# Twelve weight pieces summed from direct cast loads in the gate stage, ten in the FFN units; LN1 scaling split over engines; output stores on SP

## The chip, the cores and the metric

One Trainium2 chip, 8 NeuronCores, each running the same program on one batch element of the input. A core has TensorE (PE, matmuls, with its weight loads as PEld), VectorE (DVE), ScalarE (ACT), GpSimd (POOL) and SyncE (SP), which here only issues DMAs. DMAs issued from SP move data as they are; DMAs issued from POOL can also cast float32 to bfloat16 on the way. A time is the device time, in microseconds (us), of the slowest core.

## What is computed

One encoder layer with post-norm residuals, width 1024, 2048 tokens a core:

```python
proj = x @ w_in                    # conv input, attention q k v, memory q, 3 x 1024 gate logits
y_conv, y_attn, y_mem = conv branch, windowed attention, memory attention
gates = sigmoid(gate_logits + b_gate).reshape(B, S, 3, D)
merged = gates[:, :, 0] * y_conv + gates[:, :, 1] * y_attn + gates[:, :, 2] * y_mem
x = layer_norm(alpha * x + merged @ w_o, ln1_g, ln1_b)
gate, up = split(x @ w_ffn_in, 2)  # 2 x 2816 columns
x = layer_norm(alpha * x + (silu(gate) * up) @ w_ffn_out, ln2_g, ln2_b)
```

## The kernel before

Each engine runs its instructions in the order in which the program emits them; the small class `Eng` (line 36) adds the semaphore waits that each instruction needs. So an instruction that waits holds up all that its engine was given later, and a DMA that waits holds up the engine that issues it. Line 148 issues every DMA, line 233 every matmul.

**Stage A** (to about 320 us): input projections, convolution, both attentions and the first quarter of the gates, in an order written out by hand (`ORDER`). In it POOL also casts pieces of `w_ffn_in` from float32 to a bfloat16 copy in DRAM (`cache_w1`, `w1_bf16_cache`), 8 times one piece and then, in `load_b`, three.

**Gate stage** (lines 980 to 1013, about 320 to 583 us). `c_main(dp, tt)` lists 12 items for one quarter `dp` of the columns and one block `tt` of 512 tokens: for two column halves and three branches a gate (`c_gate`, 8 matmuls, ACT applies tanh, line 838) and an output (`c_out`, 4 matmuls, DVE multiplies out of PSUM, line 859); POOL adds the three products (lines 866 and 871). Stage A holds `dp` 0, the gate stage `dp` 1 to 3, 144 items. Ahead of each quarter POOL issues the next quarter's weights (three `w_g`, one `w_out`). PSUM has 8 banks, taken in turn; five buffers `gb` hold gates.

In between, `straight` calls `fold_step` after every 6 items. The FFN's first product is done by Strassen's scheme: a unit (128 columns) has seven matmul groups of 4 matmuls of 512 columns on seven forms of its weights. A piece comes as four quarter blocks; five more forms are sums of these. `fold_load` (SP) reloads a piece from the DRAM copy, `fold_sum` adds the forms on DVE (lines 819 to 821) and SP stores seven forms to DRAM (`w1_forms`). 22 pieces, two buffers `FG`. The copies that stage A left out are issued by `cache_w1(4)`, `(4)` and `(3)` among the weight loads.

**w_o loop** (line 1295 on, 16 blocks of 128 tokens): `d_mm` (16 matmuls), `d_H` (residual add and sum, DVE, line 1073), and a pipeline step `d_chain`, which serves five blocks at once: transposes on PE (`d_Tpe`) and their copy on ACT (`d_Tev`, line 1112), the sum of squares on ACT (`d_S`, line 1032), three tiny DVE ops (`d_tiny`, lines 1037 to 1042), the reciprocal root on POOL (`d_rstd`, line 1047), and `d_C`: LN1's centring and scaling on DVE (lines 1052 and 1054), a cast to bfloat16 on ACT (line 1092), a store of x1 to DRAM. 12 of 20 steps run here, 8 more inside FFN units 0 to 10. Then `e_sums` forms the input sums of Strassen's scheme on DVE (lines 1138 to 1142).

**FFN**, twice (two halves of 1024 tokens): 22 units `f1_unit` (even: gate, odd: up), then 8 blocks `f2_block` (44 matmuls each, then the residual, LN2 and the output store). A unit's weights come from `w1_forms` into three buffers `w1s`; `load_w1(u + 2)` is issued at the start of unit u. In a unit ACT copies three products out of PSUM (line 1172), POOL adds them twice (lines 1179 and 1183), the last four groups accumulate onto these banks, and DVE subtracts and adds out of PSUM four times (line 1193). After a gate unit ACT applies SiLU (1198, 1201 and, later, 1223, 1226); in an up unit DVE (1207, 1211) and, after the next unit's adds, POOL (1232, 1236) multiply. The order of POOL and ACT in the next unit is set by the list `late`. While units 7 to 17 run, POOL casts `w_ffn_out` in (22 loads). `load_hb` reads x1 back as the residual.

## Time and profile before

| what | us |
|---|---|
| median of 3 runs (1131.66 to 1138.48) | 1133.59 |
| the profiled execution, device time | 1130.92 |
| its span on the slowest core (core 1) | 1129.4 |
| PE busy | 985.3 (87%) |
| DVE busy | 541.1 (48%) |
| ACT busy | 396.2 (35%) |
| POOL busy | 326.9 (29%) |
| DMA queue of POOL, share of 16 engines | 27.1% |
| DMA queue of SP, share of 16 engines | 30.7% |

The spans of the eight cores lie between 1117.6 and 1129.4 us. A busy PE is a PE with matmuls in flight: how fast they go depends on the granted clock, which a table by stage shows beside the busy time (1.00 is 2.4 GHz, 0.50 is 1.2 GHz). An idle engine costs something only where the chain of work waits for it, so waits are read from the stage in which PE stops.

### The profile page before, as it was taken

To read this page: it belongs to the slowest core of one execution; us is meant where nothing else is said; L and a number is where in the kernel's file an instruction comes from. 1 tells how busy PE (TensorE), PEld (TensorE's weight loads), DVE (VectorE), ACT (ScalarE), POOL (GpSimd) and SP (SyncE) were. 2 spreads that over 40 slices of the span, in tenths; PEclk is the share of its full clock that TensorE was granted. 3 is DMA by queue.
4 is the path that set the end of the run, shared out by engine and by line. 5 is a ranking of instruction groups with operands and counts; after the bars stand their busy time and mean duration, and the time that the engine had idled before them with its cause. 6 is when DMAs were issued, how large, how long until landed. Compare 5 with 4: busy or idle time off the path is not lost.

```text
span 1129.4 us, 16455 instructions; the slowest of 8 cores (1117.6 to 1129.4 us)
## 1 busy us (share of the span) xinstructions
PE 985.3 (87%) x5606; PEld 452.3 (40%) x5606; DVE 541.1 (48%) x949; ACT 396.2 (35%) x604; POOL 326.9 (29%) x346
## 2 busy tenths in 40 slices
PE   4999999898991589289999878799999989999996
PEld 1455545444440234034444323344444434444442
DVE  2223757476611143035637964535564445545344
ACT  1136575665520112012223644444411134443011
POOL 3200001021430133033320124467731145665111
PEclk9999999999995889689999988989999989999998
DMA  9994144543499969957538533589823354442132
GB/s 129 166 175 93 44 105 70 120 67 72 73 139 159 157 198 219 168 194 245 180 137 267 187 103 135 154 216 241 216 105 112 112 183 162 139 157 66 57 112 75
DMA packets 45586, 161.15 MB, mean 143 GB/s; under 512 B 5632, under 2 KB 17544, under 8 KB 44256
## 3 DMA queue, kind: packets, MB, share of 16 engines
q1 hardware_dynamic: 32096, 110.54, 30.7%
q0 software_dynamic: 13408, 49.55, 27.1%
q8 instruction: 47, 0.77, 0.3%
q14 instruction: 35, 0.29, 0.1%
HBM read 161.32 MB, written 50.65 MB: 188 GB/s over the span
## 4 chain that ended last, share of the span: by engine, by line
PE 64%; DMA 19%; DVE 6%; issue 6%; POOL 3%; ACT 2%; SPq 1%; DVEq 0%; ACTq 0%; POOLq 0%
PE ps L233 63%; DMA w_forms<-arena 10%; DMA arena<-w_bf_cache 4%; DMA arena<-xt 2%; DVE arena L1052 2%; DVE arena L1193 2%; DMA arena<-u_scratch 1%; DMA arena<-w_forms 1%; POOL arena L1179 1%; POOL arena L1183 1%; ACT arena L1172 1%; SPq L148 1%; DVE arena L1054 1%; POOL arena L148 0%; POOL arena L1236 0%
## 5 line engine op out<-in xcount | busy, mean ns | idle before, releaser
L233 PE MATMUL ps<-arena 128*128 128x512 bf16 (+5 forms) x5196 | 969.7, 366 | 131.7 <-DVE arena L859 68.4
L233 PEld LDWEIGHTS ps<-arena 128*128 128x128 bf16 (+2 forms) x5196 | 432.1, 99 | 651.9 <-issue 212.0
L1193 DVE TENSOR_TENSOR arena<-arena,ps 128x512 f32<-128x512 f32 x176 | 114.7, 682 | 143.7 <-POOL arena L1183 141.1
L838 ACT ACTIVATE arena<-ps,bgate_sb 128x512 f32<-128x512 f32 x96 | 65.8, 687 | 239.7 <-PE ps L233 236.5
L866 POOL TENSOR_TENSOR arena<-arena 128x512 f32<-128x512 f32 x32 | 40.8, 1275 | 212.5 <-DVE arena L859 212.5
L1172 ACT COPY arena<-ps 128x512 f32<-128x512 f32 x132 | 76.2, 585 | 68.4 <-PE ps L233 63.1
L1179 POOL TENSOR_TENSOR arena<-arena 128x512 f32<-128x512 f32 x44 | 55.8, 1268 | 124.4 <-ACT arena L1172 124.3
L859 DVE SCALAR_TENSOR_TENSOR arena<-arena,ps 128x512 f32<-128x512 f32 x96 | 63.6, 681 | 52.5 <-PE ps L233 48.5
L1032 ACT ACTIVATE arena<-arena 128x1024 bf16<-128x1024 f32 x32 | 33.8, 1057 | 156.3 <-DVE arena L1259 146.7
L819 DVE TENSOR_TENSOR arena<-arena 128x1024 bf16<-128x1024 bf16 x22 | 16.4, 745 | 133.9 <-DMA arena<-w_bf_cache 133.9
L148 POOL DMA_DIRECT2D arena<-w_g x21 | 11.3, 544 | 171.1 <-PE ps L233 169.9
L1183 POOL TENSOR_TENSOR arena<-arena 128x512 f32<-128x512 f32 x44 | 55.6, 1264 | 9.1 <-POOL arena L1179 9.1
L1047 POOL TENSOR_TENSOR mvt<-mvt,eps_t 128x1 f32<-128x1 f32 x32 | 17.7, 554 | 138.4 <-DVE mvt L1042 138.4
L871 POOL TENSOR_TENSOR arena<-arena 128x512 bf16<-128x512 f32 x32 | 43.2, 1350 | 28.5 <-DVE arena L859 24.3
L645 ACT ACTIVATE arena<-ps 128x1024 bf16<-128x1024 f32 x46 | 46.6, 1025 | 12.2 <-PE ps L233 11.9
L648 DVE TENSOR_TENSOR arena<-arena 128x1024 bf16<-128x1024 bf16 x46 | 33.8, 736 | 28.4 <-ACT arena L645 28.2
L1052 DVE SCALAR_TENSOR_TENSOR arena<-arena,mvt 128x1024 f32<-128x1024 f32 x32 | 41.0, 1282 | 13.2 <-POOL mvt L1047 13.2
L1054 DVE SCALAR_TENSOR_TENSOR arena<-arena,mvt 128x1024 f32<-128x1024 f32 x32 | 41.1, 1284 | 3.8 <-DVE arena L1052 0.5
L1259 DVE SCALAR_TENSOR_TENSOR arena<-arena,ps 128x1024 f32<-128x1024 f32 x16 | 19.5, 1221 | 44.5 <-PE ps L233 44.5
L1198 ACT ACTIVATE arena<-ps 128x512 f32<-128x512 f32 x22 | 13.1, 598 | 66.6 <-DVE arena L1193 66.6
L1092 ACT CAST arena<-arena 128x1024 bf16<-128x1024 f32 x16 | 16.7, 1045 | 44.6 <-DVE mvt L1037 37.7
L352 ACT CAST arena<-ps 128x512 bf16<-128x512 f32 (+1 forms) x32 | 18.3, 571 | 38.1 <-PE ps L233 38.1
(106 smaller groups left out, 546.3 us busy)
## 6 DMA issues: line engine op xcount, KB each, us to landing
arena<-w_forms SPq DMA_DIRECT2D x44, 896.0 KB, 5.1
w_forms<-arena SPq DMA_DIRECT2D x22, 896.0 KB, 6.0
arena<-w_bf_cache SPq DMA_DIRECT2D x22, 512.0 KB, 4.3
arena<-u_scratch SPq DMA_DIRECT2D x64, 135.0 KB, 3.7
arena<-x SPq DMA_DIRECT2D x16, 512.0 KB, 9.8
x_scratch<-arena SPq DMA_DIRECT2D x16, 512.0 KB, 3.0
arena<-x_scratch SPq DMA_DIRECT2D x16, 512.0 KB, 3.8
out<-arena POOLq DMA_DIRECT2D x16, 512.0 KB, 3.0
```

Source lines behind the costliest of these rows:

```text
L233: return pe.run(lambda: nc.tensor.matmul(out, lhsT, rhs, start=start, stop=stop, skip_group_check=onto), deps, inc)
L645: t_p = act.run(lambda: nc.scalar.activation(flat, bank2(b), AF.Exp, scale=0.125), [tk, PTw_free[rp], btab["t"]])
L838: t = act.run(lambda: nc.scalar.activation(gb[r], ps[:, bk, :], AF.Tanh, bias=bgate[:, b * 8 + dc:b * 8 + dc + 1], scale=0.5), [tk, gb_fre ...
L859: t_y = dve.run(lambda: nc.vector.scalar_tensor_tensor(out=gb[r], in0=gb[r], scalar=1.0, in1=ps[:, bk, :], op0=ALU.add, op1=ALU.mult), [tk ...
L866: c_state["s"] = pool.run(lambda: nc.gpsimd.tensor_tensor(out=gb[r0], in0=gb[r0], in1=gb[r], op=ALU.add), [c_state["y", 0], t_y])
L871: t_mg[dp, tt, dci] = pool.run(lambda: nc.gpsimd.tensor_tensor(out=merged[dp][:, dci, tt * 512:(tt + 1) * 512], in0=gb[r0], in1=gb[r], op= ...
L1052: te = dve.run(lambda: nc.vector.scalar_tensor_tensor(out=buf, in0=buf, scalar=mv[:, 0:1], in1=tabs[:, 0, :], op0=ALU.subtract, op1=ALU.mu ...
L1054: return dve.run(lambda: nc.vector.scalar_tensor_tensor(out=dst, in0=buf, scalar=mv[:, 2:3], in1=tabs[:, 1, :], op0=ALU.mult, op1=ALU.add) ...
L1172: return act.run(lambda: nc.scalar.copy(dst, ps[:, b, :]), deps)
L1179: s = pool.run(lambda: nc.gpsimd.tensor_tensor(out=T3, in0=T3, in1=T4, op=ALU.add), [t3, t4])
L1183: s1 = pool.run(lambda: nc.gpsimd.tensor_tensor(out=T1, in0=T3, in1=T1, op=ALU.add), [s, t1])
L1193: return dve.run(lambda: nc.vector.tensor_tensor(out=dst, in0=dst, in1=ps[:, b, :], op=op), deps)
```

## The change

- Twelve pieces are summed in the gate stage, one per 12 items: POOL loads a piece with a cast straight from the float32 weights into SBUF, in a `w_ffn_in` layout with the four blocks reordered, issued 18 items ahead; the seven forms now fill one buffer. The other ten pieces are all copied to DRAM in stage A (8 single ones, two in `load_b`), loaded as four blocks into the unit's weight buffer, and summed there by DVE at the end of the unit two before (`fold_w1(u + 2)`), in both passes. The copies in the gate stage go.
- LN1: the centred rows y are stored to DRAM instead of x1. Centring (`d_Y`) no longer waits for the reciprocal root. Scaling writes bfloat16 directly: on DVE for every third block and for all in the FFN units, else on ACT (scale) and POOL (add of the bias). The residual of LN2 is rebuilt from y on ACT and POOL ahead of each `f2_block` (`hb_prep`).
- The chain starts a block earlier and rests once: 14 steps in the w_o loop, 6 in the units. `e_sums` stands ahead of the last `d_H`. `w_ffn_out` loads begin at unit 8.
- LN2's table goes to buffers of its own, loaded after unit 21. Output stores are issued by SP.

The diff, cut to its core (left out: declarations, the host's reordering of the blocks, `cache_w1(2)` for `(3)` in `load_b`, the counter's start at piece 12, `z_free` as the first wait of a gate buffer):

```diff
@@ -801,33 +803,38 @@

-    FG = [V(156.5 + 9 * i, [128, 9, 4, 128]) for i in range(2)]
+    FG = [V(156.5 + 7 * i, [128, 7, 4, 128]) for i in range(2)]
     fg_slot = [new_slot("fg") for _ in range(2)]
...

-    def fold_load(v):
-        if v < 22:
-            fold_ld[v] = dma(sp, FG[v % 2][:, 0:4], w1b_d[v], fg_slot[v % 2], [w1_raw[v], fold_st.get(v - 2), a_done])
-
-    def fold_sum(v):
-        G = FG[v % 2].rearrange("p s k c -> p s (k c)")
+    def fold(buf, dep):
+        G = buf.rearrange("p s k c -> p s (k c)")

...

-        dve.run(lambda: nc.vector.tensor_tensor(out=G[:, 4:6, :], in0=G[:, 0:2, :], in1=twice(3), op=ALU.add), [fold_ld[v]])
-        dve.run(lambda: nc.vector.tensor_tensor(out=G[:, 6:8, :], in0=G[:, 0:2, :], in1=twice(2), op=ALU.add))
-        t = dve.run(lambda: nc.vector.tensor_tensor(out=G[:, 8, :], in0=G[:, 3, :], in1=G[:, 2, :], op=ALU.subtract))
-        fold_st[v] = dma(sp, w1f_d[v], FG[v % 2][:, 2:9], fs_slot[v % 2], [t])
-
-    fold_n = iter(range(22))
+        t1 = dve.run(lambda: nc.vector.tensor_tensor(out=G[:, 4:6, :], in0=G[:, 2:4, :], in1=twice(0), op=ALU.add), [dep])
+        dve.run(lambda: nc.vector.tensor_tensor(out=G[:, 6, :], in0=G[:, 1, :], in1=G[:, 0, :], op=ALU.subtract))
+        return dve.run(lambda: nc.vector.tensor_tensor(out=G[:, 2:4, :], in0=G[:, 2:4, :], in1=twice(1), op=ALU.add), [t1])
+
+    def fold_load(v):
+        if v < NFOLD:
+            fold_ld[v] = dma(pool, FG[v % 2][:, 0:4], w_f1_d[v], fg_slot[v % 2], [fold_st.get(v - 2), a_done])
+
+    def fold_sum(v):
+        t = fold(FG[v % 2], fold_ld[v])
+        fold_st[v] = dma(sp, w1f_d[v], FG[v % 2], fs_slot[v % 2], [t])
+
+    fold_n = {"i": 0}

     def fold_step():
-        v = next(fold_n, None)
-        if v is not None:
-            fold_load(v + 1)
-            fold_sum(v)
+        i = fold_n["i"]
+        fold_n["i"] += 1
+        if i % 12 == 5 and i >= 12:
+            fold_load(i // 12 + 1)
+        if i % 12 == 11:
+            fold_sum(i // 12)

...
@@ -890,11 +897,11 @@

-    def straight(items, each=0):
-        for i, (_, f) in enumerate(items):
+    def straight(items, folds=False):
+        for _, f in items:
             f()
             tick()
-            if each and i % each == each - 1:
+            if folds:
                 fold_step()
...
@@ -980,18 +987,16 @@
     a_done = pe.tok()
-    cache_w1(4)
+    fold_load(0)
     t_ln1 = load(ln1t, bass.AP(ln1_d.tensor, 0, [[0, 128], [D, 2], [1, D]]), [a_done, t_sT[3, 3]], sp)
-    fold_load(0)
     load_wg(2, [pe.tok()])
     load_wos(2, [])
-    cache_w1(4)
-    straight(cat([c_main(1, tt) for tt in range(4)]), 6)
+    fold_load(1)
+    straight(cat([c_main(1, tt) for tt in range(4)]), True)
     load_wg(3, [pe.tok()])
...
     t_wo = load(w_o_sb, w_o_d, [a_done])
-    cache_w1(3)
-    straight(cat([c_main(2, tt) for tt in range(4)]), 6)
+    straight(cat([c_main(2, tt) for tt in range(4)]), True)
     dp2_done = pe.tok()
...
@@ -1000,17 +1005,24 @@
     def load_w2(j):
-        w2_tok[j] = load(w2[j], w_f2_d[:, j, :], [x1_st[j // 2 + (12 if j < 8 else 0)]])
+        w2_tok[j] = load(w2[j], w_f2_d[:, j, :], x1_free[j // 2 + (12 if j < 8 else 0)])

...
         if u < 44:
-            r = u % 3
-            w1_tok[u] = dma(sp, w1s[r], w1f_d[u % 22], w1_slot[r], [w1_free[r], fold_st[u % 22]])
-
-    straight(cat([c_main(3, tt) for tt in range(4)]), 6)
+            r, v = u % 3, u % 22
+            if v < NFOLD:
+                w1_tok[u] = dma(sp, w1s[r], w1f_d[v], w1_slot[r], [w1_free[r], fold_st[v]])
+            else:
+                w1_tok[u] = dma(sp, w1s[r][:, 0:4], w1b_d[v], w1_slot[r], [w1_free[r], w1_raw[v]])
+
+    def fold_w1(u):
+        if u < 44 and u % 22 >= NFOLD:
+            w1_tok[u] = fold(w1s[u % 3], w1_tok[u])
+
+    straight(cat([c_main(3, tt) for tt in range(4)]), True)
     c_done = pe.tok()
...
@@ -1042,17 +1054,21 @@

-    def ln_rstd(t3, k):
-        mv = mvt[:, k % 4, :]
+    def ln_rstd(t3, k, out):
         return pool.run(lambda: nc.gpsimd.tensor_tensor(
-            out=mv[:, 2:3], in0=mv[:, 1:2], in1=eps_t[:, 2:3], op=ALU.pow), [t3, t_eps])
-
-    def ln_affine(buf, tabs, dst, t_rs, k, deps=()):
-        mv = mvt[:, k % 4, :]
-        te = dve.run(lambda: nc.vector.scalar_tensor_tensor(
-            out=buf, in0=buf, scalar=mv[:, 0:1], in1=tabs[:, 0, :], op0=ALU.subtract, op1=ALU.mult), [t_rs, deps])
+            out=out, in0=mvt[:, k % 4, 1:2], in1=eps_t[:, 2:3], op=ALU.pow), [t3, t_eps])
+
+    def ln_center(buf, tab, k, deps):
         return dve.run(lambda: nc.vector.scalar_tensor_tensor(
-            out=dst, in0=buf, scalar=mv[:, 2:3], in1=tabs[:, 1, :], op0=ALU.mult, op1=ALU.add), [te])
+            out=buf, in0=buf, scalar=mvt[:, k % 4, 0:1], in1=tab, op0=ALU.subtract, op1=ALU.mult), deps)
+
+    def ln_scale(buf, dst, rs, tab, deps):
+        return dve.run(lambda: nc.vector.scalar_tensor_tensor(
+            out=dst, in0=buf, scalar=rs, in1=tab, op0=ALU.mult, op1=ALU.add), deps)
+
+    def ln_scale_ap(buf, mid, dst, rs, tab, deps):
+        t = act.run(lambda: nc.scalar.activation(mid, buf, AF.Identity, scale=rs), deps)
+        return pool.run(lambda: nc.gpsimd.tensor_tensor(out=dst, in0=mid, in1=tab, op=ALU.add), [t])

...
@@ -1082,17 +1098,30 @@

+    Z = [V(184.5 + 4 * i, [128, D], F32) for i in range(2)]
+    z_free = [None, None]
+
+    def d_Y(tb):
+        xb = X1[tb % 12]
+        d_state["y", tb] = ln_center(xb, ln1t[:, 0, :], tb, [d_state["t3", tb], t_ln1])
+        x1_st[tb] = dma(sp, y_d[tb * 128:(tb + 1) * 128, :], xb, st_slot[tb % 12], [d_state["y", tb]])
+
     def d_rstd(tb):
-        d_state["rs", tb] = ln_rstd(d_state.pop(("t3", tb)), tb)
-
-    def d_C(tb):
+        d_state["rs", tb] = ln_rstd(d_state.pop(("t3", tb)), tb, rs16[:, tb:tb + 1])
+
+    def d_C(tb, on_dve):
         xb = X1[tb % 12]
         r = tb % 3
-        t_ln = ln_affine(xb, ln1t, xb, d_state.pop(("rs", tb)), tb, [t_ln1])
-        d_state["cb", tb] = act.run(lambda: nc.scalar.copy(x1b[r], xb), [t_ln, x1b_free[r]])
+        deps = [d_state["rs", tb], d_state.pop(("y", tb)), x1b_free[r], z_free[tb % 2]]
+        rs, b1 = rs16[:, tb:tb + 1], ln1t[:, 1, :]
+        if on_dve:
+            t_ln = ln_scale(xb, x1b[r], rs, b1, deps)
+        else:
+            t_ln = ln_scale_ap(xb, Z[tb % 2], x1b[r], rs, b1, deps)
+            z_free[tb % 2] = t_ln
+        d_state["cb", tb] = t_ln
         d_state["ln"] = t_ln
-        x1_st[tb] = dma(sp, x1_d[tb * 128:(tb + 1) * 128, :], xb, st_slot[tb % 12], [t_ln])
-        x1_free[tb] = [x1_st[tb], d_state["cb", tb]]
+        x1_free[tb] = [x1_st[tb], t_ln]
         if tb + 12 < 16:
...
@@ -1239,10 +1268,12 @@

+        fold_w1(u + 2)
+
     def load_hb(tb):
...
             r = tb % 3
-            hb_tok[tb] = dma(sp, HB[r], x1_d[tb * 128:(tb + 1) * 128, :], hb_slot[r], [x1_st[tb], hb_free[r]])
+            hb_tok[tb] = dma(sp, HB[r], y_d[tb * 128:(tb + 1) * 128, :], hb_slot[r], [x1_st[tb], hb_free[r]])

...
@@ -1258,17 +1289,25 @@
             out=xb, in0=xb, scalar=ALPHA, in1=bank2(bO), op0=ALU.mult, op1=ALU.add,
-            accum_out=hsum[:, 1, tb:tb + 1]), [tk, hb_tok[tb]])
+            accum_out=hsum[:, 1, tb:tb + 1]), [tk, hb_x[tb]])
         banks.release(bO, t_h, 2)
         t_st2 = ln_stats(xb, [t_h], tb)
-        t_rs2 = ln_rstd(ln_tiny(t_st2, tb, hsum[:, 1, tb:tb + 1], 0), tb)
-        t_ln = ln_affine(xb, ln2t, xb, t_rs2, tb, [e_state["ln2"]])
-        hb_free[r] = [dma(pool, out_d[tb * 128:(tb + 1) * 128, :], xb, s_out[r], [t_ln])]
+        t3 = ln_tiny(t_st2, tb, hsum[:, 1, tb:tb + 1], 0)
+        t_rs2 = ln_rstd(t3, tb, rs16[:, 16 + tb:17 + tb])
+        t_y = ln_center(xb, ln2t[0], tb, [t3, e_state["ln2"]])
+        t_ln = ln_scale(xb, xb, rs16[:, 16 + tb:17 + tb], ln2t[1], [t_rs2, t_y])
+        hb_free[r] = [dma(sp, out_d[tb * 128:(tb + 1) * 128, :], xb, s_out[r], [t_ln])]
         load_hb(tb + 3)

+    hb_x = {}
+
+    def hb_prep(tb):
+        if tb < 16:
+            hb_x[tb] = ln_scale_ap(HB[tb % 3], HB[tb % 3], HB[tb % 3], rs16[:, tb:tb + 1], ln1t[:, 1, :], [hb_tok[tb], d_state["rs", tb]])
+
     chain = {"k": -2}

-    def d_chain():
+    def d_chain(last):
         k = chain["k"]
...
@@ -1278,31 +1317,34 @@
         if 0 <= k < 16:
-            d_C(k)
+            d_C(k, last or k % 3 == 2)
+        if 0 <= k + 1 < 16:
+            d_Y(k + 1)
+            d_rstd(k + 1)
         if k + 2 < 16:
             d_tiny(k + 2)
-        if 0 <= k + 1 < 16:
-            d_rstd(k + 1)

...
         d_mm(tb)
+        if tb == 15:
+            e_start()
+            e_sums(0, [c_done])
         d_H(tb)
-        if tb >= 2 and tb not in (5, 10):
-            d_chain()
-    e_start()
-    e_sums(0, [c_done])
+        if tb >= 1 and tb != 8:
+            d_chain(False)
     w2_order = list(range(8, 22)) + list(range(8))
...
         if u % 3 != 2 and chain["k"] < 18:
-            d_chain()
-            if chain["k"] == 18:
-                e_state["ln2"] = load(ln2t, bass.AP(ln2_d.tensor, 0, [[0, 128], [D, 2], [1, D]]), [d_state["ln"]], sp)
-        if u >= 7:
+            d_chain(True)
+        if u >= 8:
             for _ in range(2):
...
     assert chain["k"] == 18 and not w2_order
+    f1_done = [e_state["mm"]]
+    for i in range(2):
+        e_state["ln2"] = load(ln2t[i], bass.AP(ln2_d.tensor, D * i, [[0, 128], [1, D]]), f1_done, sp)
     hb_free[0] = [x1_free[11]]
...
@@ -1312,12 +1354,16 @@
                 load_hb(tb)
+            hb_prep(0)
         for tb in range(8 * P, 8 * P + 8):
+            if tb % 8 < 7:
+                hb_prep(tb + 1)
             f2_block(tb)
         if P == 0:
+            hb_prep(8)
             for u in range(22, 44):
                 f1_unit(u)
-    pool.wait([s.tok() for s in s_out])
+    sp.wait([s.tok() for s in s_out])
     return nc, {e.name: set(e.needed) for e in engines}
...
```

## Rows read from the trace of the kernel before

**Rows 1.** Busy us by stage, core 1; columns stand in the first line.

```profile
core 1: us, PE busy (x) PEld busy (x) DVE busy (x) ACT busy (x) POOL busy (x), PEclk, DMA share, GB/s
320.00:500.00 180.00, 110.69 (x476) 47.74 (x474) 43.87 (x76) 27.14 (x40) 38.33 (x38) 0.81 0.89 176
500.00:583.50 83.50, 83.50 (x388) 37.85 (x387) 43.89 (x64) 22.33 (x33) 30.57 (x23) 1.00 0.53 184
583.50:647.70 64.20, 58.63 (x320) 28.42 (x317) 48.66 (x85) 29.49 (x41) 7.30 (x12) 0.99 0.71 234
647.70:748.10 100.40, 78.20 (x336) 32.47 (x337) 53.12 (x76) 44.73 (x72) 40.66 (x39) 0.85 0.44 138
```

**Rows 2.** Waits, 320 to 584 us: us in total, times, longest us.

```profile
DVE arena L819 <- DMA arena<-w_bf_cache: 133.9, 16, 33.3
...
PE ps L233 <- DVE arena L859: 68.0, 5, 24.5
```

**Rows 3.** Order of time at one stall: start us, us, instruction [idle before].

```profile
362.59 0.69 DVE L819 TENSOR_TENSOR arena<-arena 128x1024 bf16<-128x1024 bf16 x1 [33.32 <-DMA arena<-w_bf_cache]
...
364.96 18.18 PE L233 MATMUL ps<-arena 128*128 128x512 bf16 x72 [24.47 <-DVE arena L859]
```

**Rows 4.** DMA issues, in time, and by issue (KB each, us to landing).

```profile
302.93 0.56 POOL L148 DMA_DIRECT2D arena<-w_out  x1
...
arena<-w_out POOLq DMA_DIRECT2D x1, 768.0 KB, 19.1
...
324.01 0.55 POOL L148 DMA_DIRECT2D w_bf_cache<-w_f  x1
...
w_bf_cache<-w_f POOLq DMA_DIRECT2D x1, 2048.0 KB, 73.3
...
w_forms<-arena SPq DMA_DIRECT2D x1, 896.0 KB, 32.4
arena<-w_bf_cache SPq DMA_DIRECT2D x1, 512.0 KB, 24.5
...
w_forms<-arena SPq DMA_DIRECT2D x22, 896.0 KB, 6.0
```

**Rows 5.** Order of time: sums alone, then sums that meet POOL's adds.

```profile
363.19 0.69 DVE L820 TENSOR_TENSOR arena<-arena 128x1024 bf16<-128x1024 bf16 x1
363.80 0.42 DVE L821 TENSOR_TENSOR arena<-arena 128x512 bf16<-128x512 bf16 x1
...
529.92 1.58 POOL L871 TENSOR_TENSOR arena<-arena 128x512 bf16<-128x512 f32 x1 [1.33 <-DVE arena L859]
530.29 1.76 DVE L820 TENSOR_TENSOR arena<-arena 128x1024 bf16<-128x1024 bf16 x1
...
827.59 3.35 DVE L1140 TENSOR_TENSOR arena<-arena 128x4096 bf16<-128x4096 bf16 x1
828.75 3.31 POOL L1232 TENSOR_TENSOR arena<-arena 128x512 bf16<-128x512 f32 x1
```

**Rows 6.** Order of time in one pair of FFN units.

```profile
779.18 2.67 DVE L1193 TENSOR_TENSOR arena<-arena,ps 128x512 f32<-128x512 f32 x4 [1.78 <-POOL arena L1183]
786.21 0.69 DVE L1193 TENSOR_TENSOR arena<-arena,ps 128x512 f32<-128x512 f32 x1 [4.35 <-POOL arena L1183]
...
791.14 1.26 POOL L1232 TENSOR_TENSOR arena<-arena 128x512 bf16<-128x512 f32 x1
791.27 1.28 DVE L1193 TENSOR_TENSOR arena<-arena,ps 128x512 f32<-128x512 f32 x2 [1.00 <-POOL arena L1183]
```

**Rows 7.** Waits 640 to 760 us; a group by line; order of time.

```profile
PE ps L233 <- ACT arena L1172: 21.5, 7, 4.1
...
L1092 ACT CAST arena<-arena 128x1024 bf16<-128x1024 f32 x16 | 16.7, 1045 | 44.6 <-DVE mvt L1037 37.7 <-DVE arena L1054 6.9
...
647.74 5.28 PE L233 MATMUL ps<-arena 128*128 128x512 bf16 x12 [5.62 <-ACT arena L1112]
```

**Rows 8.** Order of time in the tail.

```profile
1122.66 1.28 DVE L1052 SCALAR_TENSOR_TENSOR arena<-arena,mvt 128x1024 f32<-128x1024 f32 x1 [0.82 <-POOL mvt L1047]
```

18 lines of the change are left out of this document (10 added, 8 removed).

## The prediction

> **What bounds the kernel now.** I read the busy time by stage first, then the waits of the stage that stood out, then the order of time inside it, then the DMA issues. The table by stage [rows 1] shows two stages in which TensorE (PE) isn't the bound. From 500 us to the end of the gate stage PE is busy all of the time, 388 matmuls in 83.5 us, 0.215 us each, granted clock 1.00 (2.4 GHz). Between 320 and 500 us it is busy 110.7 of 180 us and the mean granted clock is 0.81, so part of that stretch ran at 1.2 GHz. Between 647.7 and 748.1 us (FFN units 0 to 9) it is busy 78.2 of 100.4 us at 0.85. These two stretches hold nearly all of the loss.
>
> The waits of the gate stage [rows 2] name the cause: VectorE (DVE) sat 133.9 us in front of line 819, the first weight sum of a piece, for the load of the cached weights, and PE then sat 68.0 us, in 5 stalls, behind DVE's line 859, which takes the gate outputs out of PSUM. The order of time shows one such stall [rows 3]: DVE waits 33.32 us up to 362.59, PE resumes at 364.96 after 24.47 us. DVE had stopped at 329.27, PE at 340.49: PE runs on 11.2 us on free PSUM banks before a blocked DVE costs anything. The 72 matmuls after the stall took 18.18 us, 0.2525 each: 2.7 us more than at 0.215, the price of the lower clock.
>
> Why the loads are late: the casting queue of GpSimd (POOL) is full. The w_out load issued at 302.93 landed 19.1 us later, at 322.0; the last cache copy, issued at 324.01, landed after 73.3 us, at 397.3 [rows 4]. In between the queue moved 1536 + 2048 + 1536 + 768 + 2048 KB, 7936 KB in 75.3 us, 105 KB per us. The loads of cached pieces on SP share the DMA engines with it; the one issued at 452.65 took 24.5 us and the store next to it 32.4 us [rows 4].
>
> **The change, part by part.** Gate stage. It holds 72 gates of 8 matmuls and 72 outputs of 4: 864 x 0.215 = 186 us, where before took 320.5 to 583.5, 263 us: 77 us lost. Removed: 22 reloads of 512 KB, ten stores of 896 KB, 4096 KB of cache copies around the next block's weights. Added: twelve 512 KB cast loads on POOL's queue, one per 12 items (72 matmuls, 15.5 us), issued 18 items ahead of the sum. The copies in the stage before stay as many, less one.
> New waits: POOL's load of piece v waits for the store of v-2, and POOL's gate adds queue behind that, then ACT's gates, then PE. A sum takes 0.69 + 0.42 + 0.69 = 1.8 us [rows 5], a store 6.0 us [rows 4], together 7.8, against 6 items (7.7 us) between sum and load: next to nothing except while the queue is full. It is full twice.
> First, behind w_out (322.0) lie 1024 KB of cache, piece 0, three w_g, w_out and piece 1, 4352 KB: at 105 KB per us piece 1 lands at 363.4. DVE wants it after 24 items, near 352.5. Blocked 10.9 + 1.8, less the 11.2 of PE's lead: 1.5 us, with the clock's 2.7 some 4.
> Second, after item 48 (near 387) three w_g, w_out and w_o go in front of piece 5: 4864 KB, 46 us, landing at 433; DVE wants it after item 72, near 417. 16 + 1.8 - 11.2 = 6.6, with the clock 9.
> The stage becomes 186 + 13 + 1 (a first wait for w_out, as now) = 200 us: **-63 us**. Ends: no stall at all -77; with the queue a tenth slower (94 KB per us) both stalls grow by 5 to 6 us: -51.
>
> LN1 and units 0 to 9. ACT's cast (1.045 us, 16 times) goes; about eight of the 16 scalings go to ACT (priced as that cast) and a POOL add of 128x1024, put at twice the 1.26 us of a 128x512 one, 2.5 us [rows 6, 7]. Two more chain steps stand inside the w_o loop, so 6 instead of 8 in the units; the input sums go before the last block's residual.
> In the units PE waited 21.5 us, 7 times, for line 1172, ScalarE's (ACT's) first copy of the next unit [rows 7]. That copy is queued behind the cast of the chain step, which waits for DVE's scaling. Units 0 to 9 need 280 x 0.215 = 60 us and 4 for transposes; the other 36 us belong to the sums (about 5) and 8 steps, some 4 us a step. Without the cast and its hand-overs (1.3 us) a step costs 2.7: 6 x 2.7 = 16 instead of 31. **-15 us**; ends -24 (steps nearly hidden) and -6 (only the two steps less).
> In the w_o loop (64.2 us, DVE busy 48.7 of it [rows 1]) DVE loses 8 scalings of 1.28 (10 us) [rows 8] but gets two steps more, and POOL's adds may hold it up (B below): **0**, from -8 to +8. PE's wait of 5.62 us at its end [rows 7] stays. x loads issue some 3 us later, behind the last sum and its store; PE has four blocks of banks by then.
>
> FFN, 20 of 44 units. Each folded unit adds three sums to DVE, 1.8 us, behind its last subtraction and ahead of the next unit's first. Its load shrinks from 896 to 512 KB and is due a unit earlier. In steady state a pair (gate unit, up unit) takes 791.27 - 779.18 = 12.1 us [rows 6], of which DVE works 6.7, so two folds fit by amount. The place decides. After the gate unit DVE has a gap of 4.35 us: free. After the up unit it ends at 790.27 and its next subtraction starts 1.00 us later, when POOL's two adds are done; POOL then starts two multiplications (791.14).
> There the trace shows a lock. A sum that takes 0.69 alone took 1.76 where it met a POOL add, and that add 1.58 instead of 1.26; they ran one after the other (the first of six alike) [rows 5]. The x1 sums show strict turns: DVE's 3.35, POOL's 3.31 [rows 5]. So behind an up unit the turns are sum, multiplication, sum, multiplication, sum: 0.69 + 1.26 + 0.42 + 1.26 + 0.69 = 4.3 us, from 791.2 to 795.5. The next gate unit's subtraction starts 4.2 us late, its two SiLUs and the next unit's copies on ACT follow it, and PE can give about 1 us (that gap). Some 3.1 us a pair, 10 pairs, 3 us spared at the starts of the two passes: **+28 us**. Ends: +5 (no turns: 0.5 a pair) and +38 (the gate unit's fold meets POOL too, or waits for its load).
> The Trainium skill, SBUF — State Buffer, section "SBUF: two separate sides", calls this an exclusive lock held for a whole instruction, between a DVE op with two SBUF inputs and a GpSimd op that reads SBUF. By that rule, the trace agrees (1.76 against 0.69), the time is 1079; by amounts alone it would be 1056.
>
> FFN2. LN2's centring no longer waits for the reciprocal root: 0.82 us of the tail [rows 8]. Stores go from POOL to SP, where the next residual load, which waited for them anyway, and unit 24's weights stand behind them; POOL starts unit 22's adds earlier, but the rebuild for block 8 now stands there. **-2**, from -1 to -4. Hidden: 16 residual rebuilds (1.05 ACT, 2.5 POOL) in blocks of 9.5 us (44 x 0.215), and the LN2 table's load on SP ahead of the first residual, by PE's four blocks of banks; without that cover block 0 would wait some 8 us.
>
> **Sum.** -63 - 15 + 0 + 28 - 2 = -52. The profiled execution took 1130.9 us (2.7 under the median shown, a difference left in the range): 1079.
>
> **The rivals.**
> A. The lock stays off the path: folds +5, the w_o loop gains its 8: 1079 - 23 - 8 = 1048. For it: a sum that meets no add runs at 0.69, and the phase may shift. Against: the six rows alike.
> B. The lock costs more: DVE's f32 centring and statistics take turns with the 2.5 us adds too. Each of 8 adds then holds DVE up by some 2.0, where the moved scaling saved 1.28, and the statistics wait as well: loop +8, units only -6, folds +38: 1079 + 8 + 9 + 10 = 1106. For it: the weight sums' rows. Against: no row shows such an f32 op with a pointer operand meeting a POOL add. The section named above would put these ops under the lock as well and so gives B's 1106; no run here shows it yet.
> C. Slower: the gate stage stays bound by transfers. Two buffers hold the pieces. If every piece went like the one at 452.65 (24.5 + 1.8 + 32.4 = 58.7 us), six turns of 58.7 make 352 us. The other terms sum to +11, so it decides from a stage of 252 us, 42 us a turn; at 47 us a turn it is 282: 1130.9 + 19 + 11 = 1161. Against it: a store took 6.0 us (median), and the queue carries one piece per 15 us, not four at once.
> D. Little change: B, with the slow queue (12) and a third stall of 10 where POOL waits for piece 0's store: 1128.
>
> **How the numbers follow.** Chances: forecast 0.44, A 0.23, B 0.23, C 0.04, D 0.06. The likeliest is 1079. All ends together give 1023 to 1119; the range from a little below A to a little above B holds 8 in 10: 1040 to 1112. One per cent (11 us) is about what a measurement of this kernel tells from no change. Forecast, A and B lie below 1122: faster 0.90; D: same 0.06; C: slower 0.04.
>
> **What would show it.** Gate stage: DVE's idle time for weights under 40 us instead of 134, PE's behind DVE under 15 instead of 68, at the second piece of the first block and of the second; 200 us in all. Units: no cast, PE's waits for the first copy halved. FFN: pairs of 12.1 us where nothing is folded and near 15 in units 10 to 19 and 32 to 41, the new wide sums' mean above 1.2 instead of 0.69 us, PE waiting for ACT's copies there. It would be made wrong by stalls in every gate block (C), folds that leave the pairs' time alone (A), or a w_o loop of over 72 us (B).

## The result: 1075.6 us, and where the 56 us of the profile went

| | before | after |
|---|---|---|
| median, us | 1134.21 (4 runs) | 1075.63 (4 runs) |
| ratio after / before | | 0.9476, 95% interval 0.9438 to 0.9515 |
| profiled execution | 1130.92 | 1074.63 |
| its span on the slowest core | 1129.4 (core 1) | 1073.5 (core 7) |

In some executions, whatever the kernel, the cores of one die or of both run at a lower clock; ratios leave these out, and where they shift a median by 1 us or more, the time of the profiled execution is given beside it.

The change made the kernel 5.2% faster. The forecast was 1079, with a range of 1040 to 1112. DVE's order of time has five marks that the two kernels share: the last gate output (line 859 before, 866 after), the first input sum of each pass (1138 and 1167), the read of the sum of the first FFN2 residual of the second pass (1259 and 1290), and the end of the span. Between them the time changed like this:

| stretch | before | after | change | forecast |
|---|---|---|---|---|
| to the last gate output | 583.5 | 513.0 | -70.5 | -63 |
| w_o loop, to the input sums of pass 1 | 66.3 | 72.8 | +6.5 | 0 |
| to the input sums of pass 2 | 176.7 | 171.7 | -5.0 | -15 + 14 |
| to the first residual of the second FFN2 | 226.7 | 241.9 | +15.1 | +14 |
| to the end | 76.2 | 74.3 | -2.0 | -2 |
| sum (of unrounded times) | 1129.4 | 1073.5 | -55.9 | -52 |

The busy time by stage, after, core 7 (as [rows 1]; borders at the marks, but 663.9 is about the start of unit 10 and 992.6 that of the second FFN2):

```profile
core 7: us, PE busy (x) PEld busy (x) DVE busy (x) ACT busy (x) POOL busy (x), PEclk, DMA share, GB/s
320.00:513.00 193.00, 188.70 (x866) 84.94 (x865) 78.32 (x106) 49.27 (x72) 75.04 (x69) 0.99 0.62 133
513.00:585.70 72.70, 63.93 (x343) 30.27 (x341) 60.84 (x88) 34.29 (x46) 34.54 (x21) 0.98 0.69 234
585.70:663.90 78.20, 68.05 (x320) 29.80 (x321) 53.22 (x67) 35.88 (x61) 44.00 (x34) 0.91 0.46 155
663.90:757.40 93.50, 81.38 (x352) 35.12 (x351) 72.06 (x97) 33.41 (x60) 61.33 (x57) 0.95 0.63 140
757.40:992.60 235.20, 217.41 (x976) 95.67 (x974) 149.67 (x200) 80.99 (x136) 120.67 (x85) 0.98 0.31 107
992.60:1073.50 80.90, 71.82 (x332) 32.47 (x332) 40.52 (x56) 15.97 (x22) 22.74 (x16) 0.97 0.24 85
```

In the gate stage PE is now busy 188.7 of 193 us at a clock of 0.99, where [rows 1] showed 110.7 of 180 at 0.81. What is left of the loss lies behind it: in each of the last five stages PE stands idle 9 to 18 us.

**Gate stage.** Its waits after the change (us in total, times, longest), beside [rows 2]:

```profile
POOL arena L148 <- DMA w_forms<-arena: 23.2, 4, 14.6
DVE arena L817 <- DMA arena<-w_f: 12.3, 2, 10.0
...
PE ps L234 <- DVE arena L866: 2.3, 1, 2.3
```

DVE waits 12.3 us for weights instead of 133.9, PE 2.3 behind DVE's gate outputs instead of 68.0. POOL's new wait, a piece's load behind the store of two pieces earlier, is there (23.2 us), but its longest, 14.6 us, ends at 426.2, before the load that DVE waits for lands (428.0). The order of time shows the two late pieces, and PE's one stop:

```profile
358.11 0.82 DVE L817 TENSOR_TENSOR arena<-arena 128x1024 bf16<-128x1024 bf16 x1 [2.30 <-DMA arena<-w_f]
...
428.02 0.69 DVE L817 TENSOR_TENSOR arena<-arena 128x1024 bf16<-128x1024 bf16 x1 [10.04 <-DMA arena<-w_f]
...
323.75 105.45 PE L234 MATMUL ps<-arena 128*128 128x512 bf16 x480 [2.04 <-DMA arena<-w_out]
431.46 83.90 PE L234 MATMUL ps<-arena 128*128 128x512 bf16 x388 [2.27 <-DVE arena L866]
```

They are the second piece and piece 5, the two that the forecast named, but DVE waits 2.3 and 10.0 us, not 10.9 and 16, and PE's banks cover the first wait and most of the second. After the stop 388 matmuls take 83.90 us, 0.216 each, at a granted clock of 1.00: this stop didn't lower it.

**Sums in the FFN units.** One pair, second pass: DVE's sums behind an up unit and behind the gate unit after it, POOL's two multiplications, and PE:

```profile
913.59 1.52 DVE L817 TENSOR_TENSOR arena<-arena 128x1024 bf16<-128x1024 bf16 x1
915.03 1.48 DVE L818 TENSOR_TENSOR arena<-arena 128x512 bf16<-128x512 bf16 x1
916.43 1.75 DVE L819 TENSOR_TENSOR arena<-arena 128x1024 bf16<-128x1024 bf16 x1
918.10 2.66 DVE L1222 TENSOR_TENSOR arena<-arena,ps 128x512 f32<-128x512 f32 x4
920.68 0.68 DVE L817 TENSOR_TENSOR arena<-arena 128x1024 bf16<-128x1024 bf16 x1
921.28 0.42 DVE L818 TENSOR_TENSOR arena<-arena 128x512 bf16<-128x512 bf16 x1
921.62 0.68 DVE L819 TENSOR_TENSOR arena<-arena 128x1024 bf16<-128x1024 bf16 x1
...
914.52 1.71 POOL L1261 TENSOR_TENSOR arena<-arena 128x512 bf16<-128x512 f32 x1
916.19 1.44 POOL L1265 TENSOR_TENSOR arena<-arena 128x512 bf16<-128x512 f32 x1
...
918.33 13.93 PE L234 MATMUL ps<-arena 128*128 128x512 bf16 x56 [3.01 <-DVE arena L819]
933.80 12.25 PE L234 MATMUL ps<-arena 128*128 128x512 bf16 x56 [1.55 <-DVE arena L819]
```

The same three sums take 4.6 us from first start to last end behind the up unit, in turns with POOL, and 1.6 behind the gate unit, where POOL is idle. PE resumes 0.15 us after the late sum ends. Two pairs take 949.06 - 918.33 = 30.73 us, 15.4 each, against 12.1 in [rows 6].

**w_o loop.** Of the twelve centrings of the loop (DVE, line 1062) eight take 2.98 to 3.46 us, the others 1.28. The order of time shows one of each kind, and POOL's add of the split step (1071) and its reciprocal root (1058):

```profile
559.21 1.28 DVE L1062 SCALAR_TENSOR_TENSOR arena<-arena,mvt 128x1024 f32<-128x1024 f32 x1
562.32 2.99 DVE L1062 SCALAR_TENSOR_TENSOR arena<-arena,mvt 128x1024 f32<-128x1024 f32 x1
...
561.88 2.35 POOL L1071 TENSOR_TENSOR arena<-arena 128x1024 bf16<-128x1024 f32 x1 [5.48 <-ACT arena L1070]
564.19 1.53 POOL L1058 TENSOR_TENSOR rs<-mvt,eps_t 128x1 f32<-128x1 f32 x1
```

The centring at 562.32 starts while the add runs (561.88 to 564.23), and ends 1.1 us after it. That is rival B's mechanism: 1.7 us lost, in other steps up to 2.2, where a moved scaling saved 1.28.

### The profile page after: what moved, and what is told of

Same layout as the page of the kernel before. It is cut to its first block, busy times and chain, and to the rows that moved or that the text cites. A ratio compares the mean times of both kernels' runs of the same rounds, so it can differ in the third digit from the quotient of the medians.

```text
span 1073.5 us, 16537 instructions; the slowest of 8 cores (1058.9 to 1073.5 us)
## 1 busy us (share of the span) xinstructions
PE 983.4 (92%) x5606; PEld 451.1 (42%) x5606; DVE 616.4 (57%) x971; ACT 408.4 (38%) x612; POOL 408.1 (38%) x363
## 3 DMA queue, kind: packets, MB, share of 16 engines
q1 hardware_dynamic: 29936, 90.35, 25.4%
## 4 chain that ended last, share of the span: by engine, by line
PE 66%; DVE 12%; DMA 8%; issue 6%; POOL 4%; ACT 3%; SPq 0%; DVEq 0%; POOLq 0%; ACTq 0%
PE ps L234 65%; DVE arena L1062 4%; DVE arena L1222 3%; DMA arena<-w_out 2%; DVE arena L819 2%; POOL arena L1212 1%; POOL arena L1208 1%; DMA arena<-w_q 1%; DMA arena<-xt 1%; DMA arena<-u_scratch 1%; DVE arena L1066 1%; ACT arena L1201 1%; DVE arena L817 1%; DMA gexp_scratch<-arena 1%; DMA arena<-x 1%
## 5 line engine op out<-in xcount | busy, mean ns | idle before, releaser
L845 ACT ACTIVATE arena<-ps,bgate_sb 128x512 f32<-128x512 f32 x96 | 65.6, 687 | 169.4 <-PE ps L234 158.5
L1208 POOL TENSOR_TENSOR arena<-arena 128x512 f32<-128x512 f32 x44 | 61.1, 1389 | 114.8 <-ACT arena L1201 114.8
L873 POOL TENSOR_TENSOR arena<-arena 128x512 f32<-128x512 f32 x32 | 40.8, 1274 | 97.8 <-DVE arena L866 97.7
L1071 POOL TENSOR_TENSOR arena<-arena 128x1024 f32<-128x1024 f32 (+1 forms) x24 | 59.9, 2499 | 41.8 <-ACT arena L1070 41.8
L1058 POOL TENSOR_TENSOR rs<-mvt,eps_t 128x1 f32<-128x1 f32 x32 | 26.4, 825 | 97.1 <-DVE mvt L1054 97.1
L1212 POOL TENSOR_TENSOR arena<-arena 128x512 f32<-128x512 f32 x44 | 57.9, 1316 | 9.2 <-POOL arena L1208 7.6
L1062 DVE SCALAR_TENSOR_TENSOR arena<-arena,mvt 128x1024 f32<-128x1024 f32 x32 | 59.9, 1871 | 1.7 <-DVE mvt L1054 0.2
L649 DVE TENSOR_TENSOR arena<-arena 128x1024 bf16<-128x1024 bf16 x46 | 33.8, 737 | 28.3 <-ACT arena L646 28.2
L1066 DVE SCALAR_TENSOR_TENSOR arena<-arena,rs 128x1024 f32<-128x1024 f32 (+1 forms) x24 | 45.1, 1879 | 1.7
L1070 ACT ACTIVATE arena<-arena,rs 128x1024 f32<-128x1024 f32 x24 | 27.4, 1146 | 40.4 <-DMA arena<-y_scratch 30.8
L817 DVE TENSOR_TENSOR arena<-arena 128x1024 bf16<-128x1024 bf16 x32 | 30.0, 938 | 12.3 <-DMA arena<-w_f 12.3
```

The costliest lines, as they stand in the source:

```text
L845: t = act.run(lambda: nc.scalar.activation(gb[r], ps[:, bk, :], AF.Tanh, bias=bgate[:, b * 8 + dc:b * 8 + dc + 1], scale=0.5), [tk, gb_fre ...
L1062: return dve.run(lambda: nc.vector.scalar_tensor_tensor(out=buf, in0=buf, scalar=mvt[:, k % 4, 0:1], in1=tab, op0=ALU.subtract, op1=ALU.mu ...
L1066: return dve.run(lambda: nc.vector.scalar_tensor_tensor(out=dst, in0=buf, scalar=rs, in1=tab, op0=ALU.mult, op1=ALU.add), deps)
L1071: return pool.run(lambda: nc.gpsimd.tensor_tensor(out=dst, in0=mid, in1=tab, op=ALU.add), [t])
L1208: s = pool.run(lambda: nc.gpsimd.tensor_tensor(out=T3, in0=T3, in1=T4, op=ALU.add), [t3, t4])
L1212: s1 = pool.run(lambda: nc.gpsimd.tensor_tensor(out=T1, in0=T3, in1=T1, op=ALU.add), [s, t1])
```

## The experiments

**What the unit sums cost in all.**

```diff
 def fold_w1(u):
     if u < 44 and u % 22 >= NFOLD:
-        w1_tok[u] = fold(w1s[u % 3], w1_tok[u])
+        pass
```

> The changed kernel with the 20 weight sums of the FFN units left out (the units multiply by stale forms). Theory (the sums in the units cost what the pairs grew by): a pair of units in the second half of a pass falls from 15.4 to 12.1 us, 9 pairs of 10 count, 30 us in all: 1046 us (1042 to 1052). Rival (the pairs grew because of the later loads of four blocks or of what else stands in the units): pairs stay above 14 us and the time above 1065.

Measured: 1043.3 us, ratio to before 0.9232 (0.9214 to 0.9250). Pass 1 (sums to sums) fell from 171.7 to 155.9 us, the next stretch from 241.9 to 227.1: 15.8 + 14.8 = 30.6 us for the sums of 20 units. This splits the -5.0 of pass 1: without folds it would have been -20.8, so the chain steps gave 20.8 where 15 were forecast, and the folds took 15.8 back.

**Turns with POOL, or the amount of work?**

```diff
-        w1_tok[u] = fold(w1s[u % 3], w1_tok[u])
+        w1_tok[u] = scan3(w1s[u % 3], w1_tok[u])
...
+    def scan3(buf, dep):
+        G = buf.rearrange("p s k c -> p s (k c)")
+        for i, (sl, n) in enumerate([(2, 608), (1, 344), (0, 608)]):
+            src = bass.AP(G.tensor, G[:, sl, 0:1].offset, [[G.ap[0][0], 128], [1, n]])
+            t = dve.run(lambda: nc.vector.tensor_reduce(out=mvt[:, i, 3:4], in_=src, op=ALU.add, axis=mybir.AxisListType.X),
+                        [dep] if i == 0 else ())
+        return t
```

> The changed kernel with each weight sum of the FFN units replaced, at the same place, by a DVE reduction over 608, 344 or 608 elements of the same buffer, put at 0.7, 0.4 and 0.7 us: same waits and about the same length alone, but one SBUF input instead of two (the forms are stale). Theory (turns with POOL's operations): no turns, each keeps its length beside POOL's adds, the sums behind an up unit end about 1.8 us after its last subtraction instead of 4.7, PE waits for them no longer: pairs of 12.1 to 12.6, 1049 us (1045 to 1056). Rival (the amount and the place of the work on DVE ahead of the next subtraction is what costs): pairs of 15, 1073 us (1066 to 1080).

Measured: 1043.8 us, ratio 0.9236 (0.9213 to 0.9259), where without any sums it was 1043.3; its two FFN stretches are 0.9 and 2.0 us longer than those, so some 28 of the 30.6 us are gone. The order of time behind an up unit of the second pass:

```profile
897.43 1.89 DVE L825 TENSOR_REDUCE mvt<-arena 128x1 f32<-128x608 bf16 x3
899.24 2.67 DVE L1230 TENSOR_TENSOR arena<-arena,ps 128x512 f32<-128x512 f32 x4
...
898.37 1.27 POOL L1269 TENSOR_TENSOR arena<-arena 128x512 bf16<-128x512 f32 x1
899.59 1.27 POOL L1273 TENSOR_TENSOR arena<-arena 128x512 bf16<-128x512 f32 x1
...
899.47 24.46 PE L234 MATMUL ps<-arena 128*128 128x512 bf16 x112 [0.31 <-DVE mvt L825]
924.10 24.47 PE L234 MATMUL ps<-arena 128*128 128x512 bf16 x112 [0.17 <-DVE mvt L825]
```

Three operations of 1.89 us together run through while POOL's multiplication runs at its usual 1.27. PE waits 0.17 to 0.31 us for them, and two pairs take 24.6 us. At the same place, with the same loads and a little more DVE time than 1.8 us, nearly all of the cost is gone. So neither amount nor place alone costs; two SBUF inputs beside a POOL operation do. A reduction also writes far less than a sum, but that isn't the difference: in the changed kernel DVE's 176 subtractions of line 1222, with one SBUF and one PSUM input, each write 128x512 f32 to SBUF and take 0.67 to 0.69 us, beside POOL or not. The Trainium skill, SBUF — State Buffer, section "SBUF: two separate sides", has the lock for just that kind of DVE operation against a GpSimd one, and this pair of kernels agrees: 4.6 us with two inputs, 1.9 with one.

**The same sums at another place.**

```diff
+    GS = [0] + list(range(1, 22, 2))      # summed in the gate stage
+    US = list(range(2, 22, 2))            # summed in the units
...
-            fold_ld[v] = dma(pool, FG[v % 2][:, 0:4], w_f1_d[v], fg_slot[v % 2], [fold_st.get(v - 2), a_done])
+            fold_ld[v] = dma(pool, FG[v % 2][:, 0:4], w_f1_d[GS[v]], fg_slot[v % 2], [fold_st.get(v - 2), a_done])
...
-            if v < NFOLD:
+            if v in GS:
...
-        if u < 44 and u % 22 >= NFOLD:
+        if u < 44 and u % 22 in US:
```

> The same twelve and ten pieces, chosen otherwise: the gate stage sums piece 0 and the eleven odd ones (the weights of up units), the FFN units sum the ten even ones, so that every sum in a unit stands behind a gate unit, where POOL is idle. Bytes, counts and operations stay. Theory (it is the place behind an up unit, where POOL's two multiplications start, that costs): second pass 15 us shorter (232.8 to 218), first pass 10 to 15 shorter, less in units 2 to 9 where the chain steps need DVE: 1049 us (1045 to 1056). Rival (20 sums cost by their number): the time stays, 1075 (1070 to 1080).

Measured: 1046.5 us, ratio 0.9258 (0.9238 to 0.9277). Pass 1 takes 158.5 us and the next stretch 230.1: 13.2 and 11.8 of the 30.6 us are back. The trace shows sums that meet nobody, and PE running on:

```profile
894.36 0.69 DVE L818 TENSOR_TENSOR arena<-arena 128x1024 bf16<-128x1024 bf16 x1
894.96 0.42 DVE L819 TENSOR_TENSOR arena<-arena 128x512 bf16<-128x512 bf16 x1
895.29 0.68 DVE L820 TENSOR_TENSOR arena<-arena 128x1024 bf16<-128x1024 bf16 x1
...
836.17 127.03 PE L234 MATMUL ps<-arena 128*128 128x512 bf16 x580 [2.33 <-DVE arena L820]
```

580 matmuls in 127.03 us are 0.219 each: from unit 24 to the second FFN2 PE doesn't stop. What is left of the cost, 5.6 us, is about what PE waits for the last sum: this one of 2.3 us at unit 24 and two of 4.1 us together in units 2 to 9, where the sums stand ahead of the chain steps.

**The split of LN1's scaling.**

```diff
-            d_C(k, last or k % 3 == 2)
+            d_C(k, True)
```

> The changed kernel with every LN1 scaling on DVE, none on ACT and POOL. Theory (rival B of the prediction: a split step costs DVE more by turns with POOL's 2.4 us add than the 1.28 us scaling that it saves): the w_o loop up to the input sums falls from 72.8 to 66 or 67 us, 1069 us (1066 to 1073). Rival (the split relieves DVE, which bounds the loop): DVE gets 9 scalings of 1.28 more, 12 us, less what is hidden: loop of 76 to 85 us, 1079 to 1087.

Measured: 1067.3 us, ratio 0.9447 (0.9429 to 0.9464). The loop takes 67.1 us instead of 72.8, and this tells the two apart, as the interval of the ratio overlaps that of the changed kernel; a centring and a scaling follow each other undisturbed:

```profile
561.97 1.28 DVE L1066 SCALAR_TENSOR_TENSOR arena<-arena,rs 128x1024 bf16<-128x1024 f32 x1
563.17 1.28 DVE L1062 SCALAR_TENSOR_TENSOR arena<-arena,mvt 128x1024 f32<-128x1024 f32 x1
```

A block takes 4.30 us on DVE (561.97 to 566.27), where the split took 4.84, 5.29 and 4.30 in turn. One part of the change made it slower: taking two of three scalings off DVE cost DVE time.

**The cast in the units.** One more ACT instruction where before had its cast:

```diff
         if on_dve:
             t_ln = ln_scale(xb, x1b[r], rs, b1, deps)
+            if last:
+                t_ln = act.run(lambda: nc.scalar.copy(x1b[r], x1b[r]), [t_ln])
```

> The changed kernel with one more ACT instruction in each chain step in the units: a copy of the 128 x 1024 bfloat16 block onto itself, between the scaling on DVE and the transposes, where the kernel before had its cast. Theory of the prediction (a cast and its hand-overs cost 1.3 us a step, as ACT's next copies are queued behind it): 6 steps, 8 us, in units 0 to 9 alone, PE's wait for ACT's copies there from 5 to 10 us or more: 1083 us (1080 to 1087). Rival (the units gained by having fewer steps and no wait of the cast on late scaling): 1075 to 1078.

Measured: 1078.7 us, ratio 0.9544 (0.9501 to 0.9587), between the ranges of the theory and of its rival. The expectation counted wrong: of the six steps in the units only four still scale a block, so four copies came in (1.05 us each). In the profiled execution pass 1 grew from 171.7 to 177.2 us, 1.4 a copy. PE's waits for ACT's first copy, 585 to 760 us, after and with the copies:

```profile
PE ps L234 <- ACT arena L1201: 5.1, 4, 1.9
```

```profile
PE ps L234 <- ACT arena L1203: 9.9, 5, 3.0
```

They grew by 4.8 us, while PE's waits for ACT's SiLU fell from 3.1 to 0.7. All of PE's waits in pass 1 grew by 2.1 us and its busy time by 3.4 (149.4 to 152.8), at a mean granted clock of 0.92 instead of 0.93. The price of 1.3 us for a cast and its hand-overs agrees with this profile, but it was taken of the slowest of the four executions (1083.1, the others 1077.7 to 1078.8). By the medians, 3.1 us apart on different chips, a copy costs 0.8, by the ratios to before (0.0068 apart) 1.9. So the price is of this size, and no more is shown.

**The casting queue's backlog: put back, and taken away alone.** In the changed kernel, with the copies back:

```diff
     a_done = pe.tok()
+    load(w1x_d[0:4], w_f1_d[0:4], [pe.tok()])
     fold_load(0)
...
     load_wos(2, [])
+    load(w1x_d[4:8], w_f1_d[4:8], [pe.tok()])
     fold_load(1)
...
     t_wo = load(w_o_sb, w_o_d, [a_done])
+    load(w1x_d[8:11], w_f1_d[8:11], [pe.tok()])
```

> The changed kernel with the three groups of cast copies that the kernel before issued around the gate stage's weights put back on POOL's queue, at their places, writing 2048, 2048 and 1536 KB of bfloat16 to a DRAM tensor that nobody reads. Folds, stores and the rest are the changed kernel's. Theory (the casting queue's backlog made the stalls of the kernel before): at 120 KB per us, the rate at which the second piece came in the changed kernel's trace, the second piece lands 34 us later, which costs 34 + 2 - 11 + 3 = 28, and piece 5 lands 13 us later, which costs 13 more: 1116 us (1100 to 1130), with a stall of over 20 us at the second piece. Rival (22 reloads and folds at one per 6 items, not the copies, made them): under 1090.

Measured: ratio 0.9922 (0.9877 to 0.9966), profiled execution 1123.3 us (median 1126.6). The last gate output comes at 561.9, 48.9 us later, and everything behind it takes what it took. PE's order of time:

```profile
358.12 18.04 PE L235 MATMUL ps<-arena 128*128 128x512 bf16 x72 [9.31 <-DVE arena L867]
398.07 65.16 PE L235 MATMUL ps<-arena 128*128 128x512 bf16 x288 [21.91 <-DVE arena L867]
478.49 83.86 PE L235 MATMUL ps<-arena 128*128 128x512 bf16 x379 [15.26 <-DVE arena L867]
```

Three stalls, 46.5 us; the expectation had left out that the first piece stands behind a copy too (9.3). After the first stall 72 matmuls take 18.04 us, as slow as those of [rows 3].

And the kernel before without them:

```diff
     a_done = pe.tok()
-    cache_w1(4)
...
-    cache_w1(4)
...
-    cache_w1(3)
...
-            fold_ld[v] = dma(sp, FG[v % 2][:, 0:4], w1b_d[v], fg_slot[v % 2], [w1_raw[v], fold_st.get(v - 2), a_done])
+            fold_ld[v] = dma(sp, FG[v % 2][:, 0:4], w1b_d[v % 11], fg_slot[v % 2], [w1_raw[v % 11], fold_st.get(v - 2), a_done])
```

> The kernel before without its 11 cast copies in the gate stage; the pieces are reloaded from the 11 copies that stage A made, each twice, so half of the forms are of the wrong piece. 22 reloads of 512 KB, 22 folds, one per 6 items, and 22 stores of 896 KB stay on SP. Theory (backlog of the casting queue): DVE's 133.9 us of waiting for weights falls under 30, the stage from 263 to 195 to 210 us: 1072 us (1062 to 1085). Rival (the traffic of reloads and stores, or one fold per 6 items): the stage keeps more than 235 us, 1105 or more.

Measured: 1084.5 us, ratio 0.9583 (0.9522 to 0.9643). The total is inside the theory's range, its reason isn't: the stage, 216.5 us, lies between theory and rival, the last gate output comes at 537.0, and

```profile
DVE arena L819 <- DMA arena<-w_bf_cache: 87.0, 15, 14.4
...
PE ps L233 <- DVE arena L859: 20.6, 4, 8.3
```

DVE still waits 87.0 us for weights, where under 30 were expected. So the copies are 46.5 us (583.5 to 537.0), or 48.9 seen from the changed kernel, and some 22 to 24 us of the gain belong to something else.

**What the other 22 to 24 us are: the reloads' way, or the pace?** The way alone (SP reloads, pace of the changed kernel):

```diff
-            fold_ld[v] = dma(pool, FG[v % 2][:, 0:4], w_f1_d[v], fg_slot[v % 2], [fold_st.get(v - 2), a_done])
+            fold_ld[v] = dma(sp, FG[v % 2][:, 0:4], w1b_d[12 + v % 10], fg_slot[v % 2], [w1_raw[12 + v % 10], fold_st.get(v - 2), a_done])
```

> The changed kernel with the twelve pieces of the gate stage loaded by SP from the bfloat16 copies (those of the ten cached pieces, so the forms of twelve pieces are of the wrong one) instead of by cast loads on POOL; one piece per 12 items, issued 18 items ahead, as before. The question is what the 24 us are that the gate stage still loses when only the copies are taken away (537.0 us against 513.0 at the last gate output). If it is the number and pace of the pieces: the stage stays within 5 us of the changed kernel's, 1076 us (1072 to 1081). If it is the way of the load (SP's reload next to the casts on the same DMA engines): the stage grows by 15 to 25 us, 1090 to 1100.

The pace alone (cast loads, one piece per 6 items):

```diff
-        if i % 12 == 5 and i >= 12:
-            fold_load(i // 12 + 1)
-        if i % 12 == 11:
-            fold_sum(i // 12)
+        if i % 6 == 2 and i >= 6:
+            fold_load(i // 6 + 1)
+        if i % 6 == 5 and i // 6 < NFOLD:
+            fold_sum(i // 6)
```

> The changed kernel with its twelve pieces summed one per 6 items instead of 12 (done after 72 of 144 items), each issued 9 items ahead instead of 18; loads stay cast loads on POOL. If pace is what the 24 us are: the second piece is wanted some 15 us earlier and lands where it did, DVE is blocked 18 us, PE 18 - 11 + 3 = 10, and piece 9 stands behind three w_g, w_out and w_o with 9 items of lead only, blocked 25, PE 14: 24 us in all, 1099 us (1088 to 1106). If it is the reloads' way over SP: 1076 (1072 to 1082).

Measured, way: 1072.2 us, ratio 0.9497 (0.9482 to 0.9512), last gate output at 510.8. PE never stops for a weight:

```profile
325.74 189.45 PE L234 MATMUL ps<-arena 128*128 128x512 bf16 x877 [2.74 <-DMA arena<-w_out]
```

Measured, pace: ratio 0.9754 (0.9720 to 0.9789), profiled execution 1100.0 us (median 1105.3), last gate output at 542.8, 29.8 us later:

```profile
359.86 59.69 PE L234 MATMUL ps<-arena 128*128 128x512 bf16 x268 [10.45 <-DVE arena L866]
...
442.98 102.23 PE L234 MATMUL ps<-arena 128*128 128x512 bf16 x460 [18.42 <-DVE arena L866]
```

The two stalls that were expected are there, 10.5 and 18.4 us (10 and 14 forecast); the w_o loop behind them takes 68.4 us instead of 72.8, so 25.4 us are left at the end. It is the pace: from 12 items a piece to 6 the last gate output moves by 29.8 us with cast loads (513.0 to 542.8) and by 26.2 with reloads (510.8 to 537.0), though the last of these kernels also has 22 pieces instead of 12, and number and pace weren't tried apart.

A load straight from float32 on POOL's queue, which the change's name puts first, gains nothing over a reload on SP of a copy that is there, as long as a piece has 12 items. What it saves is the making of copies: the kernel with reloads uses the ten cached pieces for twelve, so that it made no more copies, while the eleven in the gate stage of the kernel before cost 46.5 to 48.9 us.

**The output stores.**

```diff
-        hb_free[r] = [dma(sp, out_d[tb * 128:(tb + 1) * 128, :], xb, s_out[r], [t_ln])]
+        hb_free[r] = [dma(pool, out_d[tb * 128:(tb + 1) * 128, :], xb, s_out[r], [t_ln])]
...
-    sp.wait([s.tok() for s in s_out])
+    pool.wait([s.tok() for s in s_out])
```

> The changed kernel with the output stores issued by POOL again. The prediction put 2 us on the end, 0.82 of it on LN2's centring that no longer waits for the reciprocal root, and the rest on the stores' place. If the place counts, the stretch from the second FFN2's first residual to the end goes from 74.3 back to 75 or 76 us; if the centring and the order alone do it, it stays at 74.3 within 0.3. The time cannot tell these apart: 1075 to 1077 in both.

Measured: 1076.4 us, ratio 0.9533 (0.9512 to 0.9553). From the second FFN2's first residual to the end 75.2 us instead of 74.3. The last scaling, and in this kernel POOL's issue, after and with the stores back:

```profile
1068.00 1.30 DVE L1062 SCALAR_TENSOR_TENSOR arena<-arena,mvt 128x1024 f32<-128x1024 f32 x1
1069.41 1.28 DVE L1066 SCALAR_TENSOR_TENSOR arena<-arena,rs 128x1024 f32<-128x1024 f32 x1
```

```profile
1068.72 1.28 DVE L1066 SCALAR_TENSOR_TENSOR arena<-arena,rs 128x1024 f32<-128x1024 f32 x1
...
1070.56 0.58 POOL L148 DMA_DIRECT2D out<-arena  x1 [2.65 <-DVE arena L1066]
```

From the last scaling's end to the end of the span it is 2.8 us with SP (1070.69 to 1073.5) and 3.7 with POOL (1070.00 to 1073.7), as 3.7 before. So the place of the stores gives 0.9 of the 2.0 us. With the stores on POOL the stretch ahead of this one is 2.2 us longer as well (244.1), by PE's waits for ACT and POOL at the start of the second pass, but the two stretches ahead of that are 1.9 shorter; whether this is the stores' doing wasn't followed up.

**The two edits that helped, together** (e3's and e4's):

> The two helpful edits together: even pieces summed in the units and odd ones in the gate stage (1046.5 alone) and every LN1 scaling on DVE (8 us less alone). They act in different stages, so the gains add: 1038 us (1035 to 1042). Rival (with less lost in the units the w_o loop's gain is given back as a wait later, for the first units' sums next to the chain steps): 1042 to 1047.

Measured: 1041.0 us, ratio to before 0.9202 (0.9172 to 0.9233). That is 2.9% below the changed kernel (0.9202 / 0.9476 = 0.971) and beats both. The loop takes 66.5 us, pass 1 158.5, the next stretch 229.6: the gains add.

## Why the prediction was right, point by point

**Gate stage, -63 and -70.5.** The mechanism was right for the larger part: backlog of the casting queue, late weights, a blocked DVE, PE 11 us behind it; the second piece and piece 5 are the late ones. The term was mis-sized at the rate. The prediction took 105 KB per us from [rows 4]. In the changed kernel the 4352 KB ahead of and with the second piece came from 323.7 to 358.1, 126 KB per us, and the 4864 KB up to piece 5 from 388.6 to 428.0, 123. At that rate both waits fall below or near PE's lead. Why the stretch of [rows 4] was slower isn't shown. Three reloads and two stores on SP ran beside it, and 5632 of its 7936 KB were copies to DRAM, against 1024 of 4352. With the copies back and no reloads, the 8448 KB up to the second piece came at 116 (322.7 to 395.7), so the reloads and stores aren't all of it.

The prediction also gave the whole loss to the queue. The runs give it two causes of about 47 and 23 us: the copies, and a piece every 6 items with two buffers; PE's longest stops in the kernel without copies, 8.3 and 7.3 us, come while w_g, w_out and w_o are on their way. The copies cost nearly the same in either kernel (46.5 us taken out of the one, 48.9 put into the other), so the two causes add up. Two numbers of the prediction were off without bearing on the sum: the copies taken out of the stage are 5632 KB (4 + 4 + 3 pieces), not 4096, and a queue at 94 KB per us makes the two stalls 10 us longer, so the end of the term is -53, not -51.

**w_o loop, 0 and +6.5.** Here the value was wrong inside its range of -8 to +8: the prediction put the turns with POOL's adds at nothing in its forecast and left them to rival B, whose mechanism is shown: f32 centring with a pointer operand waits for POOL's add, 2.99 and 3.45 us instead of 1.28, and without the split the loop falls to 67.1.

**Units 0 to 9, -15 and about -20.8.** The size was off on the other side. The cast's price, 1.3 us, came back as 1.4 in the profile of the kernel with four copies, and as 0.8 by the medians. How the rest divides between fewer steps and the order of centring and statistics wasn't tried. Loop and units together were forecast at -15 and came to -14.3; rival B had lost in the units what it lost in the loop, and that didn't happen.

**Folds, +28 and +30.6.** The right size by the right rule: turns of sum and multiplication behind an up unit, free behind a gate unit. The step after it was wrong. The prediction let DVE's late subtraction delay SiLU and ACT's copies, and PE wait for these. PE's rows name line 819 itself, 12.1 us in 5 waits in each pass: PE had already finished the next unit on free banks, and the forms that it wants next are those of the late sum. And about 1 of a pair's 3.3 us is the clock (last section), which the term didn't have, so the right size is in part luck. Rival A is out, since the folds run in turns in each pair.

**End, -2 and -2.0.** 0.9 from the stores on SP, the rest from the centring that starts at once: before, line 1052 waited 0.82 us in [rows 8], and 1062 doesn't wait. From the last residual's start to the last scaling's end it is 6.12 us instead of 7.17.

The errors of the terms, -7.5, +6.5, -5.8 and +2.6, cancel to -4. That the total came so near is luck: it is better than its parts.

## What to carry to other kernels

Before moving an elementwise operation from DVE to POOL, look at which two-input DVE operations will run beside it: here a split that took 1.28 us off DVE put 1.7 to 2.2 us back on it. Where a two-input operation must stay, choose its place by what POOL does then; the sums of ten pieces in two passes cost 30.6 us with every second one behind an up unit, and 5.6 with all of them behind gate units. And a queue's rate read in a stall belongs to the traffic of that stall: 105 KB per us there, 123 to 126 once the traffic had changed.

## What the hardware showed that was not expected

- Turns reach f32 operations with a pointer operand, and a small one on POOL as well: the reciprocal root of 128 x 1 takes 0.55 us alone and 1.53 behind an add while DVE centres.
- A reduction with one SBUF input and a POOL multiplication with two run side by side at full speed (1.89 us for three reductions beside POOL and alone, 1.27 for the multiplication).
- A PE stop of 2.27 us in the gate stage left the clock high (0.216 us a matmul after it), and so did those of 1.55 us in the FFN pairs; after those of 3.01 us a part of the next units ran at the lower level in this trace. The busy time behind a stop of either kind (columns as in the table by stage above):

```profile
918.33:925.00 6.67, 6.67 (x24) 2.69 (x25) 3.87 (x7) 3.90 (x7) 2.14 (x2) 0.74 0.01 5
...
933.80:946.00 12.20, 12.20 (x56) 5.39 (x56) 9.19 (x15) 5.44 (x10) 7.24 (x6) 1.00 0.24 80
```

  The mean granted clock is 0.74 in the first 6.7 us after a stop of 3.01, between the levels of 1.2 and 2.4 GHz, and 1.00 after one of 1.55. But the length of the stop doesn't decide it alone: in the kernel with the stores on POOL, in that with the copies back and in that with a piece per 6 items, the first such stop of the second pass is 3.01 or 3.02 us too, and 56 matmuls take 12.25 us behind it, at the full clock (13.93 behind the others of that length). What decides isn't shown. So of a pair's 3.3 us some 2.3 are waiting (the mean of 3.01 and 1.55), and about 1 is clock.
- A 512 KB cast load lands in 5.9 us (median of twelve), a reload on SP in 4.3 before the change and 4.5 without the copies (medians too); in this stage the difference decided nothing.
